# Output projections of three attentions and of the mixing: all four chunks open at once, channel-tile pairs as the outer loop, blocks placed between the heads

## What is computed

```python
def memory_cross_attention(h, mem_n, w_q, w_k, w_v, w_o):
    ...
    o = jnp.einsum("bhsm,bmhd->bshd", p.astype(v.dtype), v).reshape(B, S, D_MODEL)
    return o @ w_o
def fox_attention(h, w_q, w_o, k, v, c_bhs):
    ...
    return out @ w_o
# in token_mixing
    merged = jax.nn.sigmoid(ga) * y_a + jax.nn.sigmoid(gb) * y_b
    return merged @ w_out
# in first_block
        x = x + memory_cross_attention(h, mem_n, mem_wq[l], mem_wk[l], mem_wv[l], mem_wo[l])
        h = rmsnorm(x, norm_ff_g[l])
        x = x + sqrelu_mlp(h, ff_w1[l], ff_w2[l])
```

## Time and profile before

| | |
|---|---|
| times of three runs | 1582.11, 1593.51, 1600.7 us |
| median | 1593.51 us |
| profiled execution, its own time | 1600.22 us |
| its span | 1598.4 us |
| TensorE / weight loads / VectorE / ScalarE busy | 94% / 80% / 69% / 43% |
| mean granted clock of TensorE | 0.951 |
| share of the chain that ended last: TensorE, VectorE, DMA, ScalarE | 82%, 8%, 5%, 3% |

### The profile page before, as it was taken

The page is one execution under the profiler, slowest core; times in us unless marked ns, Lnnn a source line. Parts: engine busy times, 40 slices in busy tenths (PEclk is TensorE's granted clock), DMA queues, the critical chain, the costliest instruction groups (busy, mean ns, idle before and its releaser), DMA issues.

```text
span 1598.4 us, 21203 instructions
## 1 busy us (share of the span) xinstructions
PE 1504.2 (94%) x8180; PEld 1280.3 (80%) x8180; DVE 1098.5 (69%) x1640; ACT 686.8 (43%) x884; POOL 30.2 (2%) x20
## 2 busy tenths in 40 slices
PE   7999869999999969998999989999999998899997
PEld 6888757888887845687888878888888876788886
DVE  4896177598777653385888677997655857767653
ACT  2320364455334333254554345554345346555542
POOL 0000000000000000000000000000002410000000
PEclk9999979999999875699999999999999998999999
DMA  7345444355776740042556864766744333545441
GB/s 263 132 160 177 154 150 151 106 185 202 276 273 229 260 177 1 0 161 95 174 197 229 279 234 157 275 245 215 278 149 173 119 99 108 196 136 186 162 164 63
DMA packets 60188, 279.26 MB, mean 175 GB/s; under 512 B 6632, under 2 KB 8105, under 8 KB 35274
## 3 DMA queue, kind: packets, MB, share of 16 engines
q1 hardware_dynamic: 56248, 270.68, 48.9%
q10 hardware_dynamic: 3858, 7.45, 1.3%
HBM read 273.89 MB, written 4.19 MB: 174 GB/s over the span
## 4 chain that ended last, share of the span: by engine, by line
PE 82%; DVE 8%; DMA 5%; ACT 3%; issue 2%; ACTq 0%; DVEq 0%; SPq 0%
PE acc L403 40%; PE acc L405 20%; PE acc L424 10%; DMA ada_w<-in_ada 4%; PE stat L545 3%; PE stat L642 2%; PE score L606 2%; DVE wsplit L1359 2%; DVE ada_w L1644 1%; PE acc L487 1%; PE turned L626 1%; DVE tsum L1508 1%; DMA raw<-in_pw 1%; PE score L803 1%; PE acc L491 1%
## 5 line engine op out<-in xcount | busy, mean ns | idle before, releaser
L403 PE MATMUL acc<-hA,wsplit 128*128 128x512 f32 x1728 | 615.4, 401 | 8.7 <-DVE hA L1496 6.7
L405 PE MATMUL acc<-hA,wsplit 128*128 128x256 f32 x1728 | 484.2, 280 | 0.0
L908 ACT ACTIVATE wsplit<-raw 128x2048 fp32r<-128x2048 f32 (+3 forms) x210 | 373.7, 1779 | 227.2 <-PE acc L405 209.8
L1359 DVE TENSOR_TENSOR wsplit<-raw,wsplit 128x2048 fp32r<-128x2048 f32 (+3 forms) x210 | 445.4, 2123 | 10.8 <-ACT wsplit L908 10.8
L403 PEld LDWEIGHTS acc<-hA,wsplit 128*128 128x128 f32 x1728 | 327.2, 189 | 89.7 <-issue 11.3
L405 PEld LDWEIGHTS acc<-hA,wsplit 128*128 128x128 f32 x1728 | 328.1, 190 | 0.3
L403 PE MATMUL acc<-hid,wsplit 128*128 128x512 f32 x864 | 304.1, 394 | 0.0
L405 PE MATMUL acc<-hid,wsplit 128*128 128x256 f32 x864 | 244.2, 283 | 0.0
L918 ACT ACTIVATE lowp<-acc 128x512 f32<-128x512 f32 (+1 forms) x126 | 74.0, 587 | 272.7 <-PE acc L405 230.5
L403 PEld LDWEIGHTS acc<-hid,wsplit 128*128 128x128 f32 x864 | 162.9, 189 | 34.2
L405 PEld LDWEIGHTS acc<-hid,wsplit 128*128 128x128 f32 x864 | 164.1, 190 | 0.3
(11 more groups left out here) (230 smaller groups left out, 1722.0 us busy)
## 6 DMA issues: line engine op xcount, KB each, us to landing
raw<-in_gu SPq DMA_DIRECT2D x44, 1024.0 KB, 4.9
ada_w<-in_ada SPq DMA_DIRECT2D x144, 256.0 KB, 4.6
raw<-in_up SPq DMA_DIRECT2D x32, 1024.0 KB, 4.9
raw<-in_down SPq DMA_DIRECT2D x32, 1024.0 KB, 4.9
raw<-in_dn SPq DMA_DIRECT2D x32, 704.0 KB, 4.1
raw<-in_pw SPq DMA_DIRECT2D x12, 1024.0 KB, 5.3
raw<-in_memk SPq DMA_DIRECT2D x8, 1024.0 KB, 4.9
raw<-in_memv SPq DMA_DIRECT2D x8, 1024.0 KB, 5.3
```

The costliest lines, as they stand in the source:

```text
L403: nc.tensor.matmul(dst.rearrange("p (s t) -> p s t", s=2), w, h, start=start, stop=False, skip_group_check=True)
L405: return nc.tensor.matmul(dst[:, 0:T], lo_w, h[:, 0, :], start=False, stop=stop, skip_group_check=True)
L908: nc.scalar.activation(wsplit[:, slot, 0, 0:elems_of(n)], raw[:, slot, 0:elems_of(n)], ACT.Copy).then_inc(S("w_hi"), 1)
L1359: V.tensor_tensor(wsplit[:, slot, 1, 0:e], raw[:, slot, 0:e], wsplit[:, slot, 0, 0:e].bitcast(F32), ALU.subtract).then_inc(S("w_lo"), 1)
```

## The change

Four stages, named in `OPEN`, are done another way. `open_acc` gives each of the four chunks one bank, with its two column halves of 256 side by side, so that all four can be open at once. `open_pair` does one channel pair for all four chunks, 16 triples, each now three matmuls of 256 columns into one place (the high weight twice). In the memory attentions the blocks of pairs 0, 1, 2 stand between scores and values of heads 1, 2, 3; in fox in heads 5, 9, 13; the last pair follows the attention. For `out` all four blocks follow each other behind `branch`. VectorE adds one PSUM row of 512 columns to x instead of two (for `out` two instructions instead of four). The `split_lo` of the projection's last chunk moves from the stage itself into head 0 of the attention (for `out` to the end of `branch`); the one for the next stage's third chunk moves behind the stage's last chunk.

```diff
+OPEN = ["memo0", "foxo", "memo1", "out"]
...
+        def open_acc(st, c):
+
+            return acc[:, (st.acc_base + c // 2) % 2, c % 2, :].rearrange("p (j t) -> p j t", j=2)
...
+            def open_pair(name, h, p, ready, after=None):
+
+                st = STAGE[name]
+                h = h if callable(h) else tile_of(h)
+                for c in range(st.chunks):
+                    slot = (st.base + c) % RING
+                    if p == 0:
+                        weights_ready(st, c)
+                        pe.wait_ge(S("acc_summed"), st.acc_base - 1 + c // 2)
+                    for kt in (2 * p, 2 * p + 1):
+                        if c == 0 and kt in ready:
+                            for sem, value in ready[kt]:
+                                pe.wait_ge(sem, value)
+                        for j in range(2):
+                            at = kt * 2 * P + j * P
+                            dst = open_acc(st, c)[:, j, :]
+                            w, lo_w = wsplit[:, slot, 0, at:at + P], wsplit[:, slot, 1, at:at + P]
+                            nc.tensor.matmul(dst, w, h(kt)[:, 0, :], start=kt == 0 and j == 0, stop=False, skip_group_check=True)
+                            nc.tensor.matmul(dst, w, h(kt)[:, 1, :], start=False, stop=False, skip_group_check=True)
+                            mm = nc.tensor.matmul(dst, lo_w, h(kt)[:, 0, :], start=False, stop=kt == KT - 1,
+                                                  skip_group_check=True)
+                    if p == PAIRS - 1:
+                        mm.then_inc(S("chunk_done"), 1)
+                        if after:
+                            after(c)
...
-                linear(name, h, ready, after=after)
+                if name in OPEN:
+                    for p in range(first, PAIRS):
+                        open_pair(name, h, p, ready, after)
+                else:
+                    linear(name, h, ready, after=after)
...
+                          leads=[begin, lambda: chunk(2, 2), lambda: chunk(3, 3)],
+                          between={p + 1: (lambda p=p: open_pair(f"memo{layer}", dest, p, ready)) for p in range(PAIRS - 1)})
+                residual(f"memo{layer}", dest, ready, f"ff{layer}", first=PAIRS - 1)
...
+                      between={4 * p + 5: (lambda p=p: open_pair("foxo", fo_tile, p, fo_ready)) for p in range(PAIRS - 1)})
+            residual("foxo", fo_tile, fo_ready, "memq1", first=PAIRS - 1)
...
-                    if st.base + known + AHEAD < N_CHUNKS:
+                    if st.base + known + AHEAD < N_CHUNKS and (name not in OPEN or 0 < known < st.chunks - 1):
                         split_lo(st, c + AHEAD, known + AHEAD)
...
+            def last_lo(name):
+
+                split_lo(STAGE[name], STAGE[name].chunks - 1, STAGE[name].chunks - 1)
...
+                    if name in OPEN:
+                        add(a, ka, 0, first, ALU.add if bias else ALU.mult).then_inc(S("acc_summed"), 1)
...
+                if name in OPEN:
+                    split_lo(st, st.chunks - 1 + AHEAD, st.chunks - 1 + AHEAD)
...
+                          between={0: lambda: last_lo(f"memo{layer}")})
...
+                      between={0: lambda: last_lo("foxo")})
...
+                   flush=lambda: (lo(KT - 1, KT - 1), last_lo("out")))
```

More of the change, by code:

```diff
@@ L558, in keep_clock, with residual @@
                     nc.tensor.matmul(turned[:, 0, :], ident_bf[:], mask_bf[:], start=True, stop=True)
-            def residual(name, h, ready, norm):
+            def residual(name, h, ready, norm, first=0):
                 per = STAGE[name].per_acc
@@ L717, in _ @@
             memory_attention(0, hA, mq0, mk0, lambda kt, at, n: mv0[:, kt, at:at + n], prob0, probT0,
-                             (S("memory_kept"), 2 * KT))
-            gb = head_base("mem0")[1]
-            residual("memo0", hM, {2 * p: [(S("att_lo"), gb + p + 1)] for p in range(PAIRS)}, "ff0")
+                             (S("memory_kept"), 2 * KT), hM)
             linear("up0", hA, pair_ready(norm_base("ff0")))
@@ L1434, in add_to_x @@
                 st = STAGE[name]
-                n = PAIRS * RESIDUALS.index(name)
+                n = PAIRS * [r for r in RESIDUALS if r not in OPEN].index(name) if name not in OPEN else 0
                 def add(a, ka, part, scalars, op):
                     par = (st.acc_base + ka) % 2
-                    halves = acc[:, par, :, part * T:(part + 1) * T]
+                    halves = open_acc(st, a) if name in OPEN else acc[:, par, :, part * T:(part + 1) * T]
                     if scalars is None:
@@ L1451, in combine @@
                     first = bias or gain
[L1452 to L1454 removed]
+                    if name in OPEN:
+                        add(a, ka, 0, first, ALU.add if bias else ALU.mult).then_inc(S("acc_summed"), 1)
+                    else:
+                        add(a, ka, 0, first, ALU.add if bias else ALU.mult).then_inc(S("x_half"), 1)
+                        wait("x_half", n + a + 1)
+                        add(a, ka, 1, gain, ALU.mult).then_inc(S("acc_summed"), 1)
                     if operand:
@@ L1775, in _ @@
                             ALU.subtract).then_inc(S("negc_ready"), 1)
-            attention("fox", 1 / 8, prob1, lambda part, at, n: fo[:, part, at:at + n, :])
+            attention("fox", 1 / 8, prob1, lambda part, at, n: fo[:, part, at:at + n, :],
+                      between={0: lambda: last_lo("foxo")})
             add_to_x("foxo", operand=("memq1", hA, lambda kt: col("memq1", kt)))
```

22 lines of the change are left out of this document (9 added, 13 removed).

## The result

| | before | changed |
|---|---|---|
| median of four runs, us | 1593.47 | 1608.8 |
| lowest and highest, us | 1582.11, 1600.7 | 1607.91, 1611.32 |
| profiled execution: time, span, us | 1600.22, 1598.4 | 1611.32, 1609.5 |
| mean granted clock there | 0.951 | 0.963 |

The account below looks back on a forecast made before the run. TensorE was taken as the bound, in fox at half clock. Memory attentions +17.8, fox -10.0 and out +5.0 gave +12.8 us on the profiled 1600.22; less the median's 6.7 us, 1606.3 us, range 1595 to 1624.

Parts of the forecast that it names:

- The matmuls: In the four stages, 256 triples become three 256-column matmuls each, still 0.347 us per triple: 0 us change.
- Rival 6: Weight loads not hidden in the four stages' triples: 256 x 0.34 = 87 us more, 1693 us; chance 0.02.
- The blocks: Between memory attention heads, waits move before the blocks, +0.35 us; the last block waits uncovered, +1.67 us, per attention.
- The ends: At memo0, foxo and memo1, chunks close close together and TensorE waits for VectorE's third and fourth additions: +5.4 us each.
- The clock at the ends: At each of three ends, TensorE's wait lets the clock fall: +1.5 us each, between 0 and 2.5.
- Fox: Fox attention: 7.2 us cost, 17.2 us gain from dense blocks raising a clock that heads hold; net -10.0 us.
- `out`: Mixing's output projection: the fourth chunk waits for its late split, about 5 us; +5.0 us, between +3.8 and +6.
- The median shown is 1593.51, 6.7 us lower; the difference carried over: Final sum: +12.8 us on the profiled 1600.22 us, less the 6.7 us by which the median is lower, gives 1606.3.
- rival 4: Three ends hidden, third and fourth additions done by T0 + 5.9 and T0 + 7.3: -7.9 us, 1585.6; chance 0.12.
- rival 2: In fox, the clock falls about two heads after each block: total +18.3 us, 1612; chance 0.22.
- rival 3: In fox, the clock falls at once after each block: total +30.0 us, 1623.5; chance 0.10.
- Rival 5: In memory attentions, the clock falls in each of four waits between blocks: 8.8 us more, 1615; chance 0.04.

Follow-up runs that it names:

- no_foxo: The change in memo0, memo1 and out, with foxo as in the kernel before: 1616.95 us, ratio 1.0127 to the kernel before.
- only_foxo: The change in foxo alone, with memo0, memo1 and out as in the kernel before: 1590.78 us, ratio 0.9969 to the kernel before.
- half_ends: Changed kernel, but only pairs 0 and 1 as blocks between heads, pairs 2 and 3 chunk by chunk afterwards, out as before: 1591.09 us, ratio 1.0024 to before.
- only_out: The change in out alone, with the other three stages as in the kernel before: 1596.0 us, ratio 1.0054 to the kernel before.
- warm_fox: Kernel before plus 96 unread bf16 matmuls of 256 columns while TensorE waits for the first fox scores: 1592.9 us, ratio 0.9985.
- heads_fill: Kernel before plus 4 unread bf16 matmuls of 256 columns in every fox head, nothing ahead of the scores: 1580.32 us, ratio 0.9947.
- fox_fill: Kernel before plus 124 unread matmuls of 256 columns ahead of the fox scores and 4 in every fox head: 1576.68 us, ratio 0.9926.

## Why the prediction was right, and where it was not

The forecast was 1606.3 us, the median is 1608.8; the range was 1595 to 1624. Its terms:

- **The matmuls, 0:** nearly right. A triple takes 0.351 us in the blocks (0.350 to 0.353 in every trace that has them), against 0.347 for the same stages before: 4 ns more, about 1 us over 256. The prediction expected that a trace could not tell such a difference from zero; it can. Rival 6 (loads not hidden, 0.69) is out.
- **The blocks, +0.35 and +1.67:** right in kind and nearly in size. The waits are 1.31, 0.98 and 0.97 us (1.45, 1.2, 1.2 forecast), the uncovered one 1.41.
- **The ends, 5.4:** right, about 5.3 by the same count. Third addition T0 + 8.4 (8.5), fourth T0 + 12.45 (12.65), free at T0 + 15.7 (15.85); idle 2.13 and 1.15 us, both released by the addition. The forecast's "2.2 and 2.7" were too much for the second in `memo0`, because the part between them ran at half clock and took 2.9 us instead of 1.4; at `memo1`, where that part ran at full clock, they are 2.13 and 2.42.
- **The clock at the ends, 1.5 each:** a mis-sized term. The clock did fall at all three. At `memo0` and in fox the slow part lay inside the wait for the fourth addition, which ends at the same time either way: `memo0` cost 7.6 us in all, against 7.4 without this term. At `memo1` it fell behind the last wait, and the norm sums took 1.5 us longer, just as forecast. In `no_foxo` the clock stayed at 1.00 over the same two waits at `memo1` (2.13 and 2.40 us). So it was 1.5 us in all, not 4.5.
- **Fox, -10.0:** right in direction, wrong in size both ways. Trace against trace it gave 15.35: at full clock heads took 2.56 us behind a block and 3.1 later, not 3.27, the clock rose one head before the block, and the end lost nothing to the clock. By the medians it gave only about 4 (only_foxo), with 10 at the edge of the interval.
- **`out`, +5.0:** right (5.6 in the trace, 6.6 alone). The wait of 5 us came in two parts, before the third chunk (2.56) and the fourth (2.52): the third chunk's split was late too.

The step that failed is the last of the sum: "The median shown is 1593.51, 6.7 us lower; the difference carried over". It took the profiled run's fox attention, all at 0.50, for that of every run. The 6.7 us were, as far as the runs show, not a constant offset but heads at full clock in the other runs, that is, part of the very gain that the change was to bring: the unchanged fox code differs by up to 18 us between three traces. Only the profiled run of each kernel shows its heads, so for the others this is inferred from their mean clocks. Measured against ordinary runs the parts are +22 without fox and -4 with it alone, +18 together; the whole is +15.3 by the medians, 10 to 24 by its interval, and the forecast said 12.8. So the fox term was about 6 us too favourable and the clock at the ends 3 us too dear, and the rest lies within the intervals.

That the sum came within 2.5 us is partly luck. The -10 for fox lay between the -15 of the two traces and the -4 of the medians, and the two errors just named have opposite signs. Two small slips of its arithmetic change nothing: the chance of "slower by over 1%" is 0.38 and a third of 0.50, 0.55 and not 0.53, and its own range reaches down to 1597.8, not 1599.

Of the rivals, 4 (the ends hidden, 1585.6) is refuted by the row of the third addition, which comes at T0 + 8.4 and not by T0 + 5.9. Its mechanism lives all the same, in half_ends: where chunks close 2.8 us apart, one of the two waits is gone. Rivals 2 and 3 (the clock falls after a block) are refuted by the window 630 to 686, at 0.99, and by 634 to 688 of `only_foxo`, at 1.00. Rival 5 is refuted by the clock of 1.00 over the blocks of the memory attention, with waits of up to 1.4 us between them. The Trainium skill (TensorE: Matmul & The Clock Gate, "HAM oscillation — how this bites in real kernels") advises to do all channel tiles of one output before a wait for a transfer; here leaving it cost nothing in clock, with waits of at most 1.41 us. The price was in another place, which the Trainium skill names too (Perfetto Trace Analysis, "Matmuls": groups should rotate through banks, so that one's evacuation overlaps the next one's matmuls). The change gives up just that at its ends. The trace shows about 5.3 us for it each time, and 1.3 when the chunks close further apart.

## What to carry to other kernels

An accumulator kept open over many blocks doesn't save the work of closing it: it heaps that work up at the end. Work out the time between the last matmuls of successive chunks and set it against what the other engines do per chunk, splits for the next stage included, since a ring's slots all come free there. And before a profiled run's slow stretch is counted as a gain, ask whether every run has it: compare the mean granted clock and the time of many runs, and look at the same unchanged code in other kernels' traces.

## What the runs showed of the hardware

- A stretch of small dependent products (64 of 128 rows or columns, with TensorE busy 57.54 of 60 us) ran at 0.50 for 12 to 77 us and came up to 1.00 at a point that differed from trace to trace: in the second head (half_ends), the third (only_out), the fifth (the changed kernel), the thirteenth (no_foxo), or not at all (before), in kernels whose code is the same up to there; in the eighth with the extra work ahead of them (warm_fox). Times of the kernel before go with the mean clock: of its runs in the last comparison, those with a mean clock of 0.953 to 0.956 took 1597 to 1600 us, those of 0.967 to 0.971 took 1580 to 1588.5.
- At 1.00 the same products held the clock with TensorE busy 82% of the time (14.02 of 17 us). Work that raises the clock late or not at all can be enough to keep it.
- Four unread bf16 matmuls of 256 columns per head (0.44 us at full clock, by the 96 that took 10.65 us in warm_fox) were followed by 1.00 from just after the second turn in heads_fill. The kernels with them in every head are 0.5% to 0.8% faster than before with more work done.
- Waits of TensorE: 1.3 to 1.4 us between dense blocks left the clock at 1.00. Waits of 1.78 us before the first turn of fox_fill, 2.13 us at the end of `memo0` and 2.60 us ahead of the fox scores were followed by 0.50, with light or little work around them. But 2.13 and 2.40 us at `memo1` of no_foxo were not, so a wait of some 2 us may or may not cost the clock:

```profile
765.00:783.00 18.00, 13.16 (x84) 11.52 (x83) 13.83 (x19) 13.75 (x16) 0.00 (x0) 1.00 0.34 117
```

- The same triple of products (512 + 256 columns, or 3 x 256 with the weights loaded again) starts every 0.347 or 0.351 us: a matmul more costs 4 ns.
